# A root on ScalarE and a reciprocal on VectorE for the two scales at a kernel's first layer boundary

## The chip, the cores and the metric

The kernel runs on one core of one Trainium2 chip. The metric is the device time of one execution in microseconds. The core has a matrix engine (TensorE, PE in the profile), three engines for elementwise work (VectorE = DVE, ScalarE = ACT, GpSimd = PoolE = POOL) and a queue that issues DMAs (SyncE = SP). Each engine runs its own instruction stream in order; they wait for each other through semaphores.

## The reference, cut to what matters

Everything is float32, 272 tokens (16 meta tokens and 256 of the input) by 1024 features. The change concerns the place between the first feed-forward part and the mixer behind it:

```python
def rmsnorm(x, g):
    y = x * lax.rsqrt(jnp.mean(x * x, axis=-1, keepdims=True) + EPS)
    return y * g

h = h + 0.5 * rmsnorm(swiglu(rmsnorm(h, gn[0]), ffn_w_in, ffn_w_out), gn[1])
u = rmsnorm(h, gn[2])
y = mlstm_mixer(u, ...)          # its first step is u @ w_in
```

Two scales per token stand between the last product of the feed-forward part and the first product of the mixer: r1, one over the root of the mean square of the feed-forward output, and r2, one over the root of the mean square of the new h. Behind the mixer come a second feed-forward part and two attention layers, which the change leaves as they are.

## The kernel before, in words

Activations lie with features on the 128 partitions, as eight tiles of 128 features by 272 tokens. Weights stream in 512 KB chunks through five buffers (`raw`); for each chunk ScalarE writes the rounded upper part (`w1`, L870, a CAST) and VectorE the rest (`w2`, L1233), and a product is three TensorE matmuls (upper by upper, upper by rest, rest by upper; L370 to L372). The order of work on each engine is the order in which its program is written out by hand: functions named `tensor`, `scalar`, `vector`, `gpsimd` and `sync`, each a straight list of stages. No scheduler moves anything.

The boundary "f0" works like this. While TensorE makes the last output tile of the feed-forward part, the squares of the others have been summed. `column_sums` (L428) lets TensorE sum over features, so that sums by token stand in PSUM. VectorE's `first_scale` adds epsilon (`sst`, L1400 and L1402), takes a reciprocal of the mean square (`inv`, L1405) and begins the second sum (`msq`, L1408). PoolE's `first_power` raises `sst` to the power -0.5 (`rst`, L1898): that is r1. VectorE's `second_scale` needs r1 to finish the mean square of the new h (`msq` L1419, `msh` L1423), and PoolE's `second_power` raises it to -0.5 (L1903, into `rst2`, which the profile calls rst too): that is r2. TensorE's `both_scales` spreads each scale over the partitions with three small transposes (`spread`, L435) and runs six matmuls on a constant tile `dz` (`dense`, L386) behind the first. Then for each of the eight feature tiles VectorE scales y (`scaled`, L1426), h is added (L1435 on VectorE for two tiles, L1909 on PoolE for six), VectorE applies r2 and the gain (`tmp`, L1462), ScalarE rounds it (`u1`, L956) and VectorE makes the rest (`u2`, L1443). TensorE's `head` (L414, L416, L419) starts on the mixer's first four weight chunks tile by tile as `u1` and `u2` come.

In the mixer's stage ScalarE copies each product out of PSUM (L972, L973, L981), VectorE runs a convolution over four taps (L1537), and ScalarE takes a Silu of it (L991).

The tiles `root`, `tmp` and `line_end` of the diff are on-chip buffers that are laid out one behind the other in the order of their creation; behind `line_end` come the overlaid buffers of the stages (the feed-forward part's `h1` and `h2`, the mixer's and the attention layers' tiles).

Of the kernel before, what the change touches and what calls it, by code (L numbers as in the profile page):

```python
# [9 lines left out]
ALU = mybir.AluOpType  # L10
# [3 lines left out]
P = 128  # L14
D = 1024
KT = D // P
# [86 lines left out]
def build(nc, xT, wst, wada, vec, cst, tab, rb, nrow, outT):  # L103
    ctx = ExitStack()
    with ctx:
        def sb(name, shape, dt=F32, c=ctx):
            return c.enter_context(nc.sbuf_tensor(name, shape, dt))
# [17 lines left out]
        msh = sb("msh", [P, 4])  # L125
        msq = sb("msq", [P, 4])
        rst2 = sb("rst2", [P, 4])
        tmp = sb("tmp", [P, 4, T])
        vc = sb("vc", [P, NVEC])
        cs = sb("cs", [P, NCONST])  # L130
# [9 lines left out]
        eps0 = sb("eps0", [P, 4])  # L140
        Bt = sb("Bt", [P, NH, 384])
        rbs = sb("rbs", [NH, 32])
        sb("line_end", [P, 32])
        ps = ctx.enter_context(nc.psum_tensor("ps", [P, 8, 512], F32))
        drt = nc.dram_tensor("bias_rows", [NH, 512], F32)
        rows_dr = nc.dram_tensor("weight_rows", [2, 2 * KT, P], F32)
# [177 lines left out]
        s_zero, s_cv, s_gate, s_acol, s_swm, s_swd, s_den, s_og = signal("zp_zeroed"), signal("conv_tap"), signal("gate_step"), signal("acol_made"), signal("sw_masked"), signal("sw_weighted"), signal("den_step"), signal("og_times_y")  # L324
        s_sb, s_max, s_rec, s_cu, s_tap, s_fin = signal("sb_made"), signal("max_made"), signal("rec_made"), signal("cu_zeroed"), signal("tap_made"), signal("out_made")
        s_vrow1 = signal("second_v_rows")

        s_eps, s_one, s_xacc, s_pow, s_bias, s_accy, s_accg = signal("eps_set"), signal("ones_set"), signal("x_sq_added"), signal("pow_made"), signal("bias_row"), signal("sq_added"), signal("sqg_added")
        s_hp, s_pad, s_nrm, s_m2, s_cp = signal("h_added_pool"), signal("pads_set"), signal("p_normalised"), signal("m2_made"), signal("conv_gated")
# [23 lines left out]
        def tensor(e):  # L353
# [183 lines left out]

            def both_scales(s, n):

                e.wait_ge(s_pow.handle, at(s_pow, ("r1", s)))  # L540
                spread(("r1", s), 6, n, rst)
                dense(6)
                e.wait_ge(s_pow.handle, at(s_pow, ("r2", s)))
                spread(("r2", s), 5, n, rst2)

            def rows_of_gains(l):
# [308 lines left out]
        def scalar(e):  # L855
# [63 lines left out]
            def ffn_out(f, s, n):  # L919
                for j in range(KT):  # L920
                    split_to(C_F[f] + 2 * NF + (NF * j + NF - 1) // 8 + NW - 1)
                    key, i, i2 = ("out", s, j), j % 4, j % 2
                    src, gain, y = out_of(key, n), gain_of(s, j), yg[:, j, 0:n]
                    proj(key)
                    if j == 0:
                        e.wait_ge(s_gh.handle, 1)
                        e.activation(sqa[:, 0, 0:n], src, ACT.Square).then_inc(*tick(s_sq, (s, 0)))
                        e.activation(sqa[:, 1, 0:n], src, ACT.Square, scale=gain).then_inc(*tick(s_sqg, (s, 0)))
                        e.mul(y, src, gain).then_inc(*reading(key))
                    elif j < KT - 1:  # L930
                        if j > 4:
                            e.wait_ge(s_accy.handle, at(s_accy, (s, j - 4)))
                        e.activation(sq[:, i, 0:n], src, ACT.Square).then_inc(*tick(s_sq, (s, j)))
                        if j > 2:
                            e.wait_ge(s_accg.handle, at(s_accg, (s, j - 2)))
                        e.activation(sqg[:, i2, 0:n], src, ACT.Square, scale=gain).then_inc(*tick(s_sqg, (s, j)))
                        e.mul(y, src, gain).then_inc(*reading(key))
                    else:
                        e.wait_ge(s_accy.handle, at(s_accy, (s, 3)))
                        e.activation(sq[:, i, 0:n], src, ACT.Square).then_inc(*tick(s_sq, (s, j)))  # L940
                        e.wait_ge(s_hy.handle, at(s_hy, (s, "hy", j)))
                        e.mul(y, src, gain).then_inc(*reading(key))
# [8 lines left out]

            def normalised(s, n):

                for k in range(KT):
                    e.wait_ge(*(read(("r2", s)) if k == KT - 1 else (s_tmp.handle, at(s_tmp, (s, k)))))
                    e.copy(u1[:, k, 0:n], tmp[:, k % 4, 0:n]).then_inc(*tick(s_u1, ("a", k)))  # L956
                    if k == 1:
                        split_to(C_A + NW - 1)
# [262 lines left out]
        def vector(e):  # L1221
# [174 lines left out]
            def first_scale(s, n, eps_of):  # L1396

                tt = sum_tiles(n)
                e.wait_ge(s_colsum.handle, at(s_colsum, ("sum", s)))
                m = e.tensor_tensor(sst[:, 0:2], ps[:, 7, 0:256:128], eps_of[:, 0:2], ALU.add)  # L1400
                if n == T:
                    m = e.tensor_tensor(sst[0:16, 2:3], ps[0:16, 7, 256:257], eps_of[0:16, 2:3], ALU.add)  # L1402
                m.then_inc(*tick(s_stat, ("sst", s)))
                e.wait_ge(s_stat.handle, at(s_stat, ("sst", s)))
                e.reciprocal(inv[:, 0:len(tt)], sst[:, 0:len(tt)]).then_inc(*tick(s_stat, ("inv", s)))  # L1405
                e.wait_ge(s_stat.handle, at(s_stat, ("inv", s)))
                for j, (a, z) in enumerate(tt):
                    m = e.tensor_scalar(msq[0:z - a, j:j + 1], ps[0:z - a, 7, 128 * j + 64:128 * j + 65], inv[0:z - a, j:j + 1],  # L1408
                                        msh[0:z - a, j:j + 1], ALU.mult, ALU.add)
                m.then_inc(*reading(("sum", s)))  # L1410

            def second_scale(s, n):

                tt = sum_tiles(n)
                e.wait_ge(s_pow.handle, at(s_pow, ("r1", s)))
                e.wait_ge(s_colsum.handle, at(s_colsum, ("sumc", s)))
                e.wait_ge(*read(("sum", s)))
                for j, (a, z) in enumerate(tt):
                    m = e.tensor_scalar(msq[0:z - a, j:j + 1], ps[0:z - a, 5, 128 * j:128 * j + 1], rst[0:z - a, j:j + 1],  # L1419
                                        msq[0:z - a, j:j + 1], ALU.mult, ALU.add)  # L1420
                m.then_inc(*reading(("sumc", s)))
                e.wait_ge(*read(("sumc", s)))
                e.tensor_scalar(msh[:, 0:len(tt)], msq[:, 0:len(tt)], EPS, None, ALU.max).then_inc(*tick(s_stat, ("max", s)))  # L1423
# [12 lines left out]

            def normalised(s, nxt, n, gain, eps_of):
                first_scale(s, n, eps_of)
                second_scale(s, n)

                def lower(k):
                    e.wait_ge(s_u1.handle, at(s_u1, (nxt, k)))
                    e.tensor_tensor(u2[:, k, 0:n], tmp[:, k % 4, 0:n], u1[:, k, 0:n].bitcast(F32), ALU.subtract).then_inc(  # L1443
                        *tick(s_u2, (nxt, k)))

                e.wait_ge(s_spread.handle, at(s_spread, ("r1", s)))
                e.wait_ge(*read(("out", s, KT - 1)))
                for k in range(KT):
                    if k == 0:
                        scaled(s, 0, n)  # L1450
                        h_added(s, 0, n)
                    if k + 1 < KT:
                        scaled(s, k + 1, n)
                        if k + 1 == 4:
                            h_added(s, 4, n)
                    if k == 0:
                        e.wait_ge(s_spread.handle, at(s_spread, ("r2", s)))
                    if k in (0, 4):
                        e.wait_ge(s_hd.handle, at(s_hd, (s, k)))
                    else:  # L1460
                        e.wait_ge(s_hp.handle, at(s_hp, (s, k)))
                    m = e.scalar_tensor_tensor(tmp[:, k % 4, 0:n], hT[:, k, OFF[s]:OFF[s] + n], gain(k), ps[:, 5, 0:n],  # L1462
                                               ALU.mult, ALU.mult)
                    if k == KT - 1:
                        m.then_inc(*reading(("r2", s)))
                    else:
                        m.then_inc(*tick(s_tmp, (s, k)))
                    if k:
                        lower(k - 1)
                lower(KT - 1)  # L1470
# [385 lines left out]
        def gpsimd(e):  # L1856
# [35 lines left out]
                    e.tensor_tensor(sqa[:, 1, 0:n], sqa[:, 1, 0:n], sqg[:, j % 2, 0:n], ALU.add).then_inc(  # L1892
                        *tick(s_accg, (s, j)))

            def first_power(s, n):
                nt = len(sum_tiles(n))
                e.wait_ge(s_stat.handle, at(s_stat, ("sst", s)))
                e.tensor_tensor(rst[:, 0:nt], sst[:, 0:nt], eps3[:, 0:nt], ALU.pow).then_inc(*tick(s_pow, ("r1", s)))  # L1898

            def second_power(s, n):  # L1900
                nt = len(sum_tiles(n))
                e.wait_ge(s_stat.handle, at(s_stat, ("max", s)))
                e.tensor_tensor(rst2[:, 0:nt], msh[:, 0:nt], eps3[:, 0:nt], ALU.pow).then_inc(*tick(s_pow, ("r2", s)))  # L1903

            def h_added(s, n, ks):
                for k in ks:
                    h = hT[:, k, OFF[s]:OFF[s] + n]
# [1 line left out]
                    e.tensor_tensor(h, h, yg[:, k, 0:n], ALU.add).then_inc(*tick(s_hp, (s, k)))  # L1909

            def boundary(s, n):
                first_power(s, n)
                second_power(s, n)
                h_added(s, n, (1, 2, 3, 5, 6, 7))

            def first_row_scale(s, t):
# [241 lines left out]
```

## Time and profile before

| | us |
|---|---|
| runs, median of 3 (lowest to highest) | 784.48 (784.39 to 786.89) |
| profiled execution | 784.16 |
| its span, first to last instruction | 782.0 |
| TensorE busy | 773.6 |
| VectorE busy | 579.5 |
| ScalarE busy | 415.2 |
| PoolE busy | 117.5 |

The profile tells when each instruction ran. Its times are microseconds from the start of the span; ends of matmuls are modelled. The chain of waits that ended last is put down to TensorE for 89% of the span, to VectorE for 5%, to ScalarE for 2% and to PoolE for 0%.

### The profile page before, as it was taken

Reading aid. Unit: us, or ns where it says so; the run is one execution under the profiler, and the core shown is the slowest. Engines: PE = TensorE matmul, PEld = TensorE weight load, DVE = VectorE, ACT = ScalarE, POOL = GpSimd, SP = SyncE. Lnnn points to the kernel's source line nnn. Section 1 sums busy time; section 2 is a strip of 40 time slices with the busy share of each in tenths; the row PEclk is TensorE's granted clock in tenths of the full one; section 3 lists DMA queues with packets and bytes.
Section 4 is the critical chain, followed back from the end, with each engine's and each line's share of the span. In section 5 each row is a group of like instructions: output and inputs, shape, how many; then the busy total and the mean of one; then the engine's idle time right before and its main releaser. Section 6 shows DMA issues by size and latency. Waiting matters only on the chain.

```text
span 782.0 us, 14582 instructions
## 1 busy us (share of the span) xinstructions
PE 773.6 (99%) x5764; PEld 731.0 (93%) x5764; DVE 579.5 (74%) x926; ACT 415.2 (53%) x731; POOL 117.5 (15%) x136
## 2 busy tenths in 40 slices
PE   9999999999999999999999999999999999999997
PEld 8999999999999999889999998889999988999985
DVE  6777767799696977588888888677676768567763
ACT  7544444445247566485445443556655557455541
POOL 3800000033230000000000000010054411035510
PEclk9999999999999999999999999999999999999999
DMA  9876667696416644478878786635474571754531
GB/s 348 302 263 245 217 236 241 217 330 204 159 55 220 209 155 141 129 260 311 291 276 289 267 289 213 229 135 188 143 237 135 163 269 40 237 182 136 156 114 54
DMA packets 46114, 161.93 MB, mean 207 GB/s; under 512 B 5168, under 2 KB 6736, under 8 KB 46048
## 3 DMA queue, kind: packets, MB, share of 16 engines
q1 hardware_dynamic: 46048, 161.01, 60.4%
q8 instruction: 46, 0.75, 0.4%
q14 instruction: 20, 0.16, 0.1%
HBM read 159.91 MB, written 1.08 MB: 206 GB/s over the span
## 4 chain that ended last, share of the span: by engine, by line
PE 89%; DVE 5%; ACT 2%; issue 2%; DMA 1%; SPq 0%; POOL 0%; DVEq 0%; POOLq 0%; ACTq 0%
PE ps L370 21%; PE ps L372 20%; PE ps L371 20%; PE ps L819 5%; PE ps L817 5%; PE ps L818 5%; PE ps L759 3%; DVE w L1233 2%; PE ps L674 1%; DVE cv L1537 1%; PE ps L618 1%; PE ps L749 1%; ACT w L870 1%; PE ps L730 1%; PE ps L739 1%
## 5 line engine op out<-in xcount | busy, mean ns | idle before, releaser
L1233 DVE TENSOR_TENSOR w<-raw,w 128x1024 fp32r<-128x1024 f32 x237 | 287.9, 1222 | 129.2 <-ACT w L870 128.9
L370 PE MATMUL ps<-u,w 128*128 128x256 f32 (+1 forms) x1275 | 364.7, 286 | 0.4 <-DVE w L1233 0.4
L372 PE MATMUL ps<-u,w 128*128 128x256 f32 (+1 forms) x1275 | 360.1, 282 | 0.0
L371 PE MATMUL ps<-u,w 128*128 128x256 f32 (+1 forms) x1275 | 359.8, 282 | 0.0
L870 ACT CAST w<-raw 128x1024 fp32r<-128x1024 f32 x237 | 246.1, 1049 | 114.8 <-PE ps L372 82.1
L370 PEld LDWEIGHTS ps<-u,w 128*128 128x128 f32 x1275 | 239.4, 188 | 5.4 <-issue 3.1
L372 PEld LDWEIGHTS ps<-u,w 128*128 128x128 f32 x1275 | 239.7, 188 | 0.0
L371 PEld LDWEIGHTS ps<-u,w 128*128 128x128 f32 x1275 | 239.5, 188 | 0.1
L1932 POOL TENSOR_SCALAR Sb<-Sb,st 128x256 f32<-128x256 f32 x32 | 45.1, 1426 | 95.1 <-DVE st L1701 95.1
L1251 DVE SCALAR_TENSOR_TENSOR acc<-adr,cact,acc 128x1024 f32<-128x1024 f32 x42 | 55.7, 1340 | 0.0
L914 ACT ACTIVATE si<-tmp 128x272 f32<-128x272 f32 (+1 forms) x40 | 17.0, 425 | 66.0 <-DVE tmp L1346 66.0
L1918 POOL TENSOR_TENSOR rst<-sst,eps 128x1 f32<-128x1 f32 x8 | 4.4, 555 | 313.6 <-DVE sst L1760 313.6
L370 PE MATMUL ps<-h,w 128*128 128x272 f32 x176 | 50.8, 289 | 0.0
L371 PE MATMUL ps<-h,w 128*128 128x272 f32 x176 | 50.6, 288 | 0.0
L372 PE MATMUL ps<-h,w 128*128 128x272 f32 x176 | 50.6, 288 | 0.0
L817 PE MATMUL ps<-w,h 128*128 128x512 f32 x88 | 34.4, 390 | 0.0
L819 PE MATMUL ps<-w,h 128*128 128x512 f32 x88 | 34.3, 389 | 0.0
L818 PE MATMUL ps<-w,h 128*128 128x512 f32 x88 | 34.3, 389 | 0.0
L370 PEld LDWEIGHTS ps<-h,w 128*128 128x128 f32 x176 | 33.1, 188 | 0.1
L371 PEld LDWEIGHTS ps<-h,w 128*128 128x128 f32 x176 | 33.1, 188 | 0.0
L372 PEld LDWEIGHTS ps<-h,w 128*128 128x128 f32 x176 | 33.1, 188 | 0.0
L1350 DVE TENSOR_TENSOR hf<-si,ps 128x272 f32<-128x272 f32 (+1 forms) x40 | 17.2, 431 | 19.8 <-ACT si L914 19.8
(269 smaller groups left out, 975.8 us busy)
## 6 DMA issues: line engine op xcount, KB each, us to landing
raw<-wst SPq DMA_DIRECT2D x245, 512.0 KB, 4.4
adr<-wada SPq DMA_DIRECT2D x48, 512.0 KB, 3.7
Bt<-bias_rows SPq DMA_DIRECT2D x8, 192.0 KB, 4.1
hT<-xT SPq DMA_DIRECT2D x4, 272.0 KB, 4.3
sq<-nrow SPq DMA_DIRECT2D x2, 512.0 KB, 4.7
g2row<-weight_rows SPq DMA_DIRECT2D x2, 512.0 KB, 5.8
sq<-weight_rows SPq DMA_DIRECT2D x2, 512.0 KB, 5.4
outT<-hT SPq DMA_DIRECT2D x4, 256.0 KB, 2.0
```

The source lines that it names most:

```text
L370: e.matmul(out, a, x1, start=first, stop=False)
L371: e.matmul(out, a, x2, start=False, stop=False)
L372: return e.matmul(out, b, x1, start=False, stop=last)
L759: m = e.matmul(ps[:, b, :], xx[:, kt, 128 * t:128 * t + 128], ww, start=kt == 0 and i == 0, stop=kt == 7 and i == 2)
L817: e.matmul(out, x, a, start=i == 0, stop=False)
L818: e.matmul(out, x, b, start=False, stop=False)
L819: e.matmul(out, y, a, start=False, stop=i == n - 1).then_inc(*tick(s_proj, ("tok", s, i, t, hf)))
L870: e.copy(a, r).then_inc(*tick(s_upper, k))
L1233: e.tensor_tensor(b, r, a.bitcast(F32), ALU.subtract).then_inc(*tick(s_split, k))
L1251: e.scalar_tensor_tensor(a, w, x, a, ALU.mult, ALU.add).then_inc(*tick(s_acc, k))
L1350: e.tensor_tensor(hf[f][:, i, :], gate, out_of(ku, n), ALU.mult).then_inc(*reading(ku))
L1932: e.tensor_scalar(Sb[l][:, h % 4, t, :], Sb[l][:, h % 4, t, :], st_[l][:, h % 4, 4 + t:5 + t], None, ALU.mult).then_inc(*tick(s_nrm, (l, h ...
```

## The change

The two powers leave PoolE. r1 and r2 are each made by a square root on ScalarE (into a new tile `root`) and a reciprocal on VectorE. The widths of `column_sums` stay as they are. ScalarE also takes the root of a column of ones, behind the output tile before the last one; a table load stands ahead of it. VectorE's reciprocal for r2 stands in its stream behind the first `scaled`. PoolE keeps the six additions to h. The later boundaries keep their powers.

```diff
+        root = sb("root", [P, 12])
         tmp = sb("tmp", [P, 4, T])
...
-        sb("line_end", [P, 32])
+        sb("line_end", [P, 20])
...
             def both_scales(s, n):
-                e.wait_ge(s_pow.handle, at(s_pow, ("r1", s)))
+                e.wait_ge(s_scale.handle, at(s_scale, ("r1", s)))
                 spread(("r1", s), 6, n, rst)
                 dense(6)
-                e.wait_ge(s_pow.handle, at(s_pow, ("r2", s)))
+                e.wait_ge(s_scale.handle, at(s_scale, ("r2", s)))
                 spread(("r2", s), 5, n, rst2)
...
+                        if j == KT - 2:
+                            e.wait_ge(s_one.handle, at(s_one, "sums"))
+                            e.activation(root[:, 8:9], sums[:, 0:1], ACT.Sqrt)
...
             def normalised(s, n):
+                nt = len(sum_tiles(n))
+                e.wait_ge(s_stat.handle, at(s_stat, ("sst", s)))
+                e.activation(root[:, 0:nt], sst[:, 0:nt], ACT.Sqrt).then_inc(*tick(s_root, ("r1", s)))
+                e.wait_ge(s_stat.handle, at(s_stat, ("max", s)))
+                e.activation(root[:, 4:4 + nt], msh[:, 0:nt], ACT.Sqrt).then_inc(*tick(s_root, ("r2", s)))
...
                 e.reciprocal(inv[:, 0:len(tt)], sst[:, 0:len(tt)]).then_inc(*tick(s_stat, ("inv", s)))
+                e.wait_ge(s_root.handle, at(s_root, ("r1", s)))
+                e.reciprocal(rst[:, 0:len(tt)], root[:, 0:len(tt)]).then_inc(*tick(s_scale, ("r1", s)))
...
                     if k == 0:
                         scaled(s, 0, n)
+                        e.wait_ge(s_root.handle, at(s_root, ("r2", s)))
+                        tt = len(sum_tiles(n))
+                        e.reciprocal(rst2[:, 0:tt], root[:, 4:4 + tt]).then_inc(*tick(s_scale, ("r2", s)))
                         h_added(s, 0, n)
...
             def boundary(s, n):
-                first_power(s, n)
-                second_power(s, n)
                 h_added(s, n, (1, 2, 3, 5, 6, 7))
```

ScalarE's stream before, from the output tile before the last one (`yg`, L937) to the mixer's first convolution result (`qk`, L991). In brackets stand the semaphores that an instruction waits for.

```order
L937 ACTIVATE yg<-ps,gh 128x272
L870 CAST w<-raw 128x1024 [waits proj_done,raw_landed3]
L870 CAST w<-raw 128x1024 [waits proj_done,raw_landed4]
L940 ACTIVATE sq<-ps 128x272 [waits sq_added,proj_done]
L942 ACTIVATE yg<-ps,gh 128x272 [waits hy_made]
L956 CAST u<-tmp 128x272 [waits tmp_made] x2
...
L981 COPY vT<-ps 128x272 [waits proj_done] x2
L991 ACTIVATE qk<-cv,vc 128x272 [waits conv_tap]
```

The same stretch of ScalarE's stream now.

```order
L939 ACTIVATE yg<-ps,gh 128x272
L942 ACT_TABLE_LOAD
L942 ACTIVATE root<-sums 128x1 [waits ones_set]
L872 CAST w<-raw 128x1024 [waits proj_done,raw_landed3]
L872 CAST w<-raw 128x1024 [waits proj_done,raw_landed4]
L945 ACTIVATE sq<-ps 128x272 [waits sq_added,proj_done]
L947 ACTIVATE yg<-ps,gh 128x272 [waits hy_made]
L961 ACTIVATE root<-sst 128x3 [waits norm_step]
L963 ACTIVATE root<-msh 128x3 [waits norm_step]
L966 CAST u<-tmp 128x272 [waits tmp_made] x2
...
L991 COPY vT<-ps 128x272 [waits proj_done] x2
L1001 ACT_TABLE_LOAD
L1001 ACTIVATE qk<-cv,vc 128x272 [waits conv_tap]
```

Two table loads and three roots have come in; the second load, back to the Silu's table, stands ahead of the wait for the convolution, not behind it.

VectorE's stream before, from `inv` to the second `tmp`.

```order
L1405 RECIPROCAL inv<-sst 128x3
L1408 TENSOR_SCALAR msq<-ps,inv,msh 128x1 x2
L1408 TENSOR_SCALAR msq<-ps,inv,msh 16x1
L1419 TENSOR_SCALAR msq<-ps,rst,msq 128x1 x2
L1419 TENSOR_SCALAR msq<-ps,rst,msq 16x1
L1423 TENSOR_SCALAR msh<-msq 128x3
L1426 TENSOR_TENSOR yg<-yg,ps 128x272
L1435 TENSOR_TENSOR hT<-hT,yg 128x272
L1426 TENSOR_TENSOR yg<-yg,ps 128x272
L1462 SCALAR_TENSOR_TENSOR tmp<-hT,vc,ps 128x272
L1426 TENSOR_TENSOR yg<-yg,ps 128x272
```

The same stretch now (`rst` in the second of the two new rows is `rst2`).

```order
L1415 RECIPROCAL inv<-sst 128x3
L1417 RECIPROCAL rst<-root 128x3
L1420 TENSOR_SCALAR msq<-ps,inv,msh 128x1 x2
L1420 TENSOR_SCALAR msq<-ps,inv,msh 16x1
L1431 TENSOR_SCALAR msq<-ps,rst,msq 128x1 x2
L1431 TENSOR_SCALAR msq<-ps,rst,msq 16x1
L1435 TENSOR_SCALAR msh<-msq 128x3
L1438 TENSOR_TENSOR yg<-yg,ps 128x272
L1465 RECIPROCAL rst<-root 128x3
L1447 TENSOR_TENSOR hT<-hT,yg 128x272
L1438 TENSOR_TENSOR yg<-yg,ps 128x272
L1477 SCALAR_TENSOR_TENSOR tmp<-hT,vc,ps 128x272
```

One reciprocal stands ahead of the first `msq`, and one between the first `scaled` and the first addition to h; the rest is as it was.

## Rows read from the trace of the kernel before

**Rows 1.** The page, part 1: busy time, share of span, instructions by engine.

```profile
PE 773.6 (99%) x5764; PEld 731.0 (93%) x5764; DVE 579.5 (74%) x926; ACT 415.2 (53%) x731; POOL 117.5 (15%) x136
```

**Rows 2.** PE's list of waits: who waited for whom, us, times, longest.

```profile
PE ps L435 <- POOL rst L1903: 0.5, 1, 0.5
```

**Rows 3.** PE's timeline, the boundary: start, length, line, operation, count, [idle before].

```profile
213.01 0.59 PE L435 MATMUL ps<-cs,rst 128*128 128x128 f32 x3
213.52 0.98 PE L386 MATMUL ps<-dz 128*128 128x256 f32 x6
215.00 0.59 PE L435 MATMUL ps<-cs,rst 128*128 128x128 f32 x3 [0.49 <-POOL rst L1903]
...
216.62 0.52 PE L414 MATMUL ps<-u,w 128*128 128x272 f32 x2
...
217.67 0.77 PE L419 MATMUL ps<-u,w 128*128 128x272 f32 x4
```

**Rows 4.** POOL's timeline, the boundary.

```profile
211.79 0.86 POOL L1898 TENSOR_TENSOR rst<-sst,eps 128x3 f32<-128x3 f32 x1 [8.20 <-DVE sst L1402]
214.09 0.85 POOL L1903 TENSOR_TENSOR rst<-msh,eps 128x3 f32<-128x3 f32 x1 [1.43 <-DVE msh L1423]
...
216.55 0.77 POOL L1909 TENSOR_TENSOR hT<-hT,yg 128x272 f32<-128x272 f32 x1 [0.52 <-DVE yg L1426]
```

**Rows 5.** DVE's timeline, the boundary.

```profile
211.75 0.17 DVE L1405 RECIPROCAL inv<-sst 128x3 f32<-128x3 f32 x1
...
213.17 0.64 DVE L1419 TENSOR_SCALAR msq<-ps,rst,msq 128x1 f32<-128x1 f32 x3 [0.57 <-PE ps L428]
213.84 0.17 DVE L1423 TENSOR_SCALAR msh<-msq 128x3 f32<-128x3 f32 x1
213.92 0.44 DVE L1426 TENSOR_TENSOR yg<-yg,ps 128x272 f32<-128x272 f32 x1
...
214.76 0.43 DVE L1426 TENSOR_TENSOR yg<-yg,ps 128x272 f32<-128x272 f32 x1
215.62 0.50 DVE L1462 SCALAR_TENSOR_TENSOR tmp<-hT,vc,ps 128x272 f32<-128x272 f32 x1 [0.44 <-PE ps L435]
216.04 0.43 DVE L1426 TENSOR_TENSOR yg<-yg,ps 128x272 f32<-128x272 f32 x1
...
216.79 0.82 DVE L1443 TENSOR_TENSOR u<-tmp,u 128x272 fp32r<-128x272 f32 x1
```

**Rows 6.** ACT's timeline: the boundary, ahead of it, and the mixer's stage.

```profile
203.17 1.05 ACT L870 CAST w<-raw 128x1024 fp32r<-128x1024 f32 x1 [1.15 <-PE ps L372]
...
216.15 0.42 ACT L956 CAST u<-tmp 128x272 fp32r<-128x272 f32 x1 [4.78 <-DVE tmp L1462]
...
230.29 0.68 ACT L981 COPY vT<-ps 128x272 f32<-128x272 f32 x2
232.49 0.53 ACT L991 ACTIVATE qk<-cv,vc 128x272 f32<-128x272 f32 x1 [1.52 <-DVE cv L1537]
...
247.21 1.28 ACT L987 ACT_TABLE_LOAD   x1
248.50 0.43 ACT L987 ACTIVATE g<-g 8x272 f32<-8x272 f32 x1
```

**Rows 7.** Groups of ACT by shape: count, busy us, mean ns, idle before.

```profile
L880 ACT ACTIVATE tmp<-vc 128x8 f32<-128x8 f32 x1 | 0.2, 209 | 2.5 <-DMA vc<-vec 2.5
```

**Rows 8.** The chain that ended last, 226 to 284 us: start, length, what.

```profile
227.74 1.06 ACT w L870
...
281.28 1.38 PE ps L618 x10
```

**Rows 9.** Groups of PE: 5.0 to 6.4 us, 560 to 640 us, the whole span.

```profile
L386 PE MATMUL ps<-dz 128*128 128x256 f32 x14 | 1.8, 283 | 0.0
...
L371 PE MATMUL ps<-u,w 128*128 128x256 f32 x158 | 44.1, 279 | 0.0
...
L370 PE MATMUL ps<-h,w 128*128 128x272 f32 x176 | 50.8, 289 | 0.0
```

More of the change, by code:

```diff
@@ L326, in build @@
         s_vrow1 = signal("second_v_rows")
+        s_root, s_scale = signal("root_made"), signal("scale_made")
         s_eps, s_one, s_xacc, s_pow, s_bias, s_accy, s_accg = signal("eps_set"), signal("ones_set"), signal("x_sq_added"), signal("pow_made"), signal("bias_row"), signal("sq_added"), signal("sqg_added")
@@ L1414, in second_scale @@
                 tt = sum_tiles(n)
-                e.wait_ge(s_pow.handle, at(s_pow, ("r1", s)))
+                e.wait_ge(s_scale.handle, at(s_scale, ("r1", s)))
                 e.wait_ge(s_colsum.handle, at(s_colsum, ("sumc", s)))
@@ L1893, in squares @@
                         *tick(s_accg, (s, j)))
[L1895 to L1903, printed above, removed]
             def h_added(s, n, ks):
```

## The prediction

> **What bounds the kernel now.** I read the page's busy times first. TensorE is busy for 773.6 of 782.0 us [rows 1], so an edit on other engines counts only where TensorE stands still or where it is fed late. Next comes the list of what TensorE waited for: the boundary's second spread waited 0.5 us, once, for PoolE's power [rows 2]. That is the wait which the change is about, and it caps what the step itself can give. Then I went through the boundary engine by engine. TensorE ends its six `dz` matmuls at 213.52 + 0.98 = 214.50 and starts the spread of r2 at 215.00, 0.49 idle, released by the power [rows 3]. The power itself runs from 214.09 for 0.85 [rows 4]. VectorE has `msh` done at 213.84 + 0.17 = 214.01, does one `scaled`, an addition and a second `scaled`, and then waits 0.44 for the spread until the first `tmp` at 215.62 [rows 5]. ScalarE rounds it from 216.15 [rows 6], and the head starts at 216.62 [rows 3].
>
> Behind that the head is fed, not limited by TensorE: the matmuls on the first rest, L419 at 217.67, start when `u2` ends at 216.79 + 0.82 = 217.61 [rows 3, 5]. That `u2` ends 0.29 behind PoolE's addition (216.55 + 0.77 = 217.32) [rows 4, 5], and that addition follows the third `scaled` (216.04 + 0.43) by 0.08. So what arrives earlier at the first `tmp` is handed on through `scaled`, PoolE's addition and `u2` to TensorE. Last, the chain of waits leaves TensorE at the head's end, goes through ScalarE and VectorE from 227.74 and comes back at 281.28 [rows 8]: that stretch of the mixer has no slack to hide a later ScalarE or VectorE.
>
> **The first scale.** The power for r1 goes: 211.79 to 212.65 [rows 4]. In its place ScalarE can start the root when PoolE could, 211.79. No root is in the trace. The nearest row is a Tanh of 128x8 at 209 ns [rows 7]; the far bound is an 8x272 operation at 0.43 [rows 6]. With 0.21 the root is there at 212.00, the reciprocal at 0.17, as `inv` takes [rows 5], ends at about 212.2. The first three `msq` stand behind it now and end some 0.25 later than 212.60, where they ended before (213.17 less the idle 0.57) [rows 5]. The next `msq` waits for column sums until 213.17, so this is hidden, with 0.3 to spare; with the far bound 0.1 is left. TensorE's first spread starts at 213.01 with no idle time ahead of it [rows 3], behind the column sums; r1 is ready 0.4 before. Value: nothing on either side. If the column sums were shorter, the 0.25 would show.
>
> **The second scale.** The root can start at 214.04, 0.03 behind `msh`. ScalarE is free then: it idled 4.78 up to 216.15 [rows 6]. It ends at 214.25. The reciprocal stands behind the first `scaled`, which ends at 213.92 + 0.44 = 214.36 [rows 5]; instructions there start up to 0.08 before the one ahead ends (216.04 against 215.62 + 0.50). So it runs 214.28 to 214.45, and the spread could start 0.05 later, as it did behind the power: 214.50, just when the `dz` matmuls end. The spread moves by 0.50, and the `tmp` could move by as much. But VectorE has one instruction more: the second `scaled`, 214.76 to 215.19 before, ends 0.05 to 0.17 later, and `tmp` can start at 215.15 to 215.28 instead of 215.62. That is a gain of 0.34 to 0.47. With the far bound of 0.43 for the root, the reciprocal ends at 214.67 and the gain is 0.28. It cannot turn into a loss: root and reciprocal even then take 0.68 with the hand-over, the power and its hand-over 0.91. I take 0.40. By the cycle above it reaches the head's end and the mixer's chain whole.
>
> **The table loads.** A load takes 1.28, and the operation behind it starts 0.01 after it [rows 6]. The first new load and the dummy root (1.28 + 0.21 = 1.49) stand where ScalarE idled 1.15 ahead of the CAST at 203.17 [rows 6], which moves by 0.34. Its chunk is used several chunks later, and the CAST was waiting for a buffer, so nothing is behind it: zero. Without that cover it would be 0.34. The second load goes between the copies of V, which end at 230.97, and the first Silu at 232.49, ahead of which ScalarE idled 1.52 for the convolution [rows 6]. 1.28 fits, with 0.24 left. The load has no semaphore to wait for, so I take zero. If that cover went, all of the 1.28 would go down the chain to 281.28 [rows 8].
>
> The Trainium skill ("ScalarE: Activation LUTs", section "What ACT_TABLE_LOAD costs") gives 1283 ns for the load and about 1380 ns of drain with it, 2.66 us for a switch. The trace agrees on the load and shows no drain (247.21 + 1.28 to 248.50). By the page's sum the second switch would not fit into 1.52, 1.14 would be left over, and the time would be 785.7.
>
> **The layout.** This is the part that the words of the change do not name. All buffers behind `line_end` begin 32 bytes past a multiple of 64 now. The largest group concerned on TensorE is `h` as the moving operand: 176 matmuls in each of three lines, 528 [rows 9]. What such an address costs has one witness: `dz`, which begins 32 bytes past a multiple of 64 before too. Its 128x256 matmuls last 283 ns, those on `u` 279 [rows 9]. So the bounds are 0 and 528 x 4 ns = 2.1 us. But `dz` is both operands of its matmul at once, which may be all of the 4 ns. Below nothing I see no more than some tenths: the mixer's `SW` and `Vs` tiles come to the better address, in the 10 matmuls of a head [rows 8] at 4 ns, eight heads, 0.3. I take 1 ns each, 0.5: it is a real difference between rows, and most of it may belong to `dz` alone.
>
> The Trainium skill ("SBUF — State Buffer", section "Specifications (TRN2)") gives on-chip lines of 16 bytes. By that a shift of 32 bytes would cost nothing, and the time would be 784.1; the 283 against 279 does not bear it out, unless `dz` is special.
>
> **The sum.** -0.40 for the second scale, 0 for the first, 0 for the loads, +0.5 for the layout: +0.1 on the profiled execution, whose 784.16 (span 782.0 and 2.16 around it) is 0.32 below the median of the runs, 784.48. Predicted: 784.6, no change. Its own range is 783.8 to 785.4.
>
> **Rivals.**
> *The address costs in full.* Place: the 528 matmuls of the first feed-forward part's output. For it: 283 against 279. Against: `dz` is no ordinary matmul. Price: 2.1 - 0.4, slower by 1.7, 786.2. From 0.8 ns each it outweighs the gain; from 5 ns each it would be over 0.3%, which is more than the row shows but other buffers move as well.
> *The second table load is not hidden.* Place: ahead of the first Silu. For it: only 0.24 of cover is left, and the chain behind has no slack. Against: the load waits for nothing and ScalarE was idle. Price: 1.28 if all shows, 785.9.
> *The gain alone.* The address does nothing or helps, and the gain comes whole: 784.48 - 0.5 less up to 0.3, 783.7. For it: the waits at 215.00 and 215.62 are plain. Against: the same 283.
> *The change gains nothing.* VectorE's in-order reciprocal waits for a root later than 214.9. Then 784.5 to 785.0; no row has such a long small operation.
>
> **How the numbers follow.** Chances: forecast 0.62, with the case of no gain in it; full address cost 0.20; load not hidden 0.08; gain alone 0.10. Some 0.3%, 2.4 us, is what a measurement of this kernel can tell from no change. Of the full address cost I put 0.07 above that bound, of the load 0.02; of the gain alone 0.03 below it. So faster 0.03, same 0.88, slower 0.09. The range leaves out a tenth on either side: from 783.4 (the gain alone with a little more) to 786.4 (the address in full).
>
> **What would show it.** The second spread starts within 0.1 of the end of the first `dz` group, and the first `tmp` 0.3 to 0.5 earlier against the first column sums. The reload of the Silu's table lies wholly in ScalarE's idle time ahead of the first `qk`. The matmuls of the group on `h` last 289 or some ns more: that is the layout's term, to be read in the stretch of the first feed-forward output. I am wrong if that stretch moves by more than 2 us, if the wait behind the convolution grows, or if the median leaves 783.4 to 786.4.

## The result and the profile after

| | before | after |
|---|---|---|
| median of all runs beside each other | 784.29 (783.93 to 786.89, 20 runs) | 786.82 (786.10 to 788.51, 20 runs) |
| profiled execution | 784.16 | 786.17 |
| its span | 782.0 | 784.2 |
| TensorE busy | 773.6 | 776.3 |

The changed kernel is slower by 2.53 us, a ratio of 1.0029 [1.0023, 1.0035]. That is above the forecast of 784.6 and just outside its range of 783.4 to 786.4. Executions of one kernel differ by up to some 2 us among themselves in the first 18 us of the span, ahead of all that the change touches: in two traces of one and the same kernel, the changed one with its layout put back, the same matmul starts at 18.34 and at 20.30. What follows therefore goes by the lengths of stretches in the traces and by the intervals of the ratios.

The boundary itself did what was forecast. TensorE's timeline of the changed kernel there (start, length, line, operation, count, [idle before]), to be held against [rows 3]:

```profile
213.31 0.59 PE L437 MATMUL ps<-cs,rst 128*128 128x128 f32 x3
213.82 0.98 PE L388 MATMUL ps<-dz 128*128 128x256 f32 x6
214.81 0.59 PE L437 MATMUL ps<-cs,rst 128*128 128x128 f32 x3
...
216.44 0.52 PE L416 MATMUL ps<-u,w 128*128 128x272 f32 x2
...
217.49 0.76 PE L421 MATMUL ps<-u,w 128*128 128x272 f32 x4
```

The second spread carries no bracket any more: it starts as the `dz` group ends (213.82 + 0.98 = 214.80). From the first spread to the second it is 1.50 now, 1.99 before [rows 3]; to the head's start 3.13, 3.61 before. VectorE's timeline of the changed kernel:

```profile
212.28 0.18 DVE L1417 RECIPROCAL rst<-root 128x3 f32<-128x3 f32 x1
...
213.47 0.64 DVE L1431 TENSOR_SCALAR msq<-ps,rst,msq 128x1 f32<-128x1 f32 x3 [0.49 <-PE ps L430]
214.15 0.17 DVE L1435 TENSOR_SCALAR msh<-msq 128x3 f32<-128x3 f32 x1
...
214.59 0.17 DVE L1465 RECIPROCAL rst<-root 128x3 f32<-128x3 f32 x1
...
215.06 0.43 DVE L1438 TENSOR_TENSOR yg<-yg,ps 128x272 f32<-128x272 f32 x1
215.44 0.50 DVE L1477 SCALAR_TENSOR_TENSOR tmp<-hT,vc,ps 128x272 f32<-128x272 f32 x1
```

The first `tmp` follows `msh` by 1.29, before by 1.78 [rows 5], and the 0.44 ahead of it are gone. ScalarE's timeline of the changed kernel, from the first table load to the first Silu:

```profile
202.31 1.28 ACT L942 ACT_TABLE_LOAD   x1
203.60 0.20 ACT L942 ACTIVATE root<-sums 128x1 f32<-128x1 f32 x1
203.71 1.03 ACT L872 CAST w<-raw 128x1024 fp32r<-128x1024 f32 x1
...
212.05 0.20 ACT L961 ACTIVATE root<-sst 128x3 f32<-128x3 f32 x1 [0.37 <-DVE sst L1412]
214.35 0.20 ACT L963 ACTIVATE root<-msh 128x3 f32<-128x3 f32 x1 [2.10 <-DVE msh L1435]
...
230.09 0.68 ACT L991 COPY vT<-ps 128x272 f32<-128x272 f32 x2
230.79 1.28 ACT L1001 ACT_TABLE_LOAD   x1
232.29 0.52 ACT L1001 ACTIVATE qk<-cv,vc 128x272 f32<-128x272 f32 x1 [0.21 <-DVE cv L1552]
```

A root takes 0.20. The Silu still waits 0.21 for the convolution behind the second load, so that load costs nothing.

The loss stands elsewhere. PE's groups by shape over the whole span, in the kernel before (line, operation, tiles, shapes, count | busy us, mean ns of one | idle before):

```profile
L817 PE MATMUL ps<-w,h 128*128 128x512 f32 x88 | 34.4, 390 | 0.0
L819 PE MATMUL ps<-w,h 128*128 128x512 f32 x88 | 34.3, 389 | 0.0
...
L818 PE MATMUL ps<-w,m 128*128 128x512 f32 x64 | 24.9, 389 | 0.0
L759 PE MATMUL ps<-side,u 128*128 128x512 f32 x84 | 20.5, 395 | 0.7 <-issue 0.7
...
L818 PE MATMUL ps<-w,y 128*128 128x512 f32 x32 | 12.5, 390 | 0.0
...
L674 PE MATMUL ps<-w,u 128*128 128x512 f32 x48 | 11.9, 399 | 0.0
...
L759 PE MATMUL ps<-last_side,u 128*128 128x512 f32 x12 | 3.4, 391 | 0.0
```

The same view of the changed kernel, with the group on `h` that answers to [rows 9]:

```profile
L372 PE MATMUL ps<-h,w 128*128 128x272 f32 x176 | 51.0, 290 | 0.0
...
L819 PE MATMUL ps<-w,h 128*128 128x512 f32 x88 | 34.9, 396 | 0.0
L821 PE MATMUL ps<-w,h 128*128 128x512 f32 x88 | 34.8, 396 | 0.0
...
L820 PE MATMUL ps<-w,m 128*128 128x512 f32 x64 | 25.3, 395 | 0.0
L761 PE MATMUL ps<-side,u 128*128 128x512 f32 x84 | 20.8, 398 | 0.4 <-issue 0.4
L820 PE MATMUL ps<-w,y 128*128 128x512 f32 x32 | 12.6, 395 | 0.0
...
L761 PE MATMUL ps<-last_side,u 128*128 128x512 f32 x12 | 3.5, 396 | 0.0
```

These are the products of the second feed-forward part (`w,h`: `h` is the stationary operand, `w` the moving one), of the attention layers (`w,m`), of the mixer (`w,y`) and those with the weights kept in `side`: 264 + 192 + 96 + 96 = 648 matmuls of 512 columns. Each is 3 to 6 ns longer. No engine's wait explains it: the groups have no idle time ahead of them in either kernel, but for `side`, whose idle time shrank from 0.7 to 0.4. What differs is where `h`, `m`, `y` and `side` lie.

Holding the start of every matmul in one trace against its start in the other, from 18 us on, the stretches change by: `w,h` +1.68; `w,m` +1.21; `w,y` +0.31; `side` and `last_side` +0.38; `h,w` +0.21; the boundary -0.49; a wait for weights ahead of `side` -0.27; `u,w` -1.06. That is +2.0, as much as the two profiled executions are apart (786.17 - 784.16).

### The profile page after: what moved, and what is told of

Its sections match the earlier page's. It is cut to its first block, busy times and chain, and to the rows that moved or that the text cites. A ratio compares the mean times of both kernels' runs of the same rounds, so it can differ in the third digit from the quotient of the medians.

```text
span 784.2 us, 14587 instructions
## 1 busy us (share of the span) xinstructions
PE 776.3 (99%) x5764; PEld 730.7 (93%) x5764; DVE 579.5 (74%) x928; ACT 418.1 (53%) x736; POOL 116.2 (15%) x134
## 4 chain that ended last, share of the span: by engine, by line
PE 89%; DVE 5%; ACT 3%; issue 2%; DMA 0%; DVEq 0%; POOLq 0%; POOL 0%; SPq 0%; ACTq 0%
PE ps L372 21%; PE ps L373 20%; PE ps L374 20%; PE ps L821 5%; PE ps L819 5%; PE ps L820 5%; PE ps L761 3%; DVE w L1243 2%; PE ps L676 1%; DVE cv L1552 1%; PE ps L620 1%; ACT w L872 1%; PE ps L751 1%; PE ps L732 1%; PE ps L741 1%
```

## The experiments

Two things were to be told apart first: the change at the boundary and the layout. Then there were two theories of the layout: a matmul is longer when an operand's own address is no multiple of 64 bytes, or the distance between its two operands' addresses decides. Last, which part of the edit at the boundary gives the gain.

Addresses below are bytes per partition, modulo 256. Before: `w1`, `w2`, `h`, `m`, `y` at 0, `side` at 64, `u` at 64 where it is read from token 16 on (256 and 512 columns) and at 0 where all 272 tokens are read. After: `h`, `m`, `y` at 32, `side` at 96. "Distance" is the moving operand's address less the stationary one's, again modulo 256; that 256 is the right period is not shown.

### The changed kernel with the layout put back

```diff
-        sb("line_end", [P, 20])
+        sb("line_end", [P, 16])
```

> The changed kernel with line_end at 64 bytes, so that all buffers behind it lie where they lay before; roots, reciprocals and table loads stay. Theory A (the loss is the layout: 264 matmuls on h, 192 on m, 96 on y and 96 on side, 512 columns wide, each 5 to 6 ns longer, 3 to 3.5 us in all) expects 783.8, 0.4 to 0.5 faster than before, and 389 to 390 ns for these matmuls. Theory B (the loss is the new table loads or the waits for ScalarE) expects 786.8, as the changed kernel.

Measured: 783.66 (783.39 to 786.26, 11 runs) beside 784.71 for the kernel before, ratio 0.9994 [0.9984, 1.0005]. One buffer that nobody reads is 16 bytes shorter (32 in the built program), `tmp` and its neighbours still lie higher, and the loss is gone. This was run a second time on another chip, together with the changed kernel as it is:

> The changed kernel with line_end at 16 floats a row, so that everything laid out behind it stands where it stood, a second time, beside the changed kernel itself, for a tighter comparison. The theory (the boundary gains 0.48 us, the rest is as before): 783.6 to 783.9 us, 0.4 to 0.7 below the kernel before. The rival (the boundary's gain is lost again further on): within 0.2 us of the kernel before.

> The changed kernel unedited, on the same chip as its version with the layout put back. The theory (the layout costs 2.8 to 3.2 us beside a gain of 0.48): 786.4 to 786.9 us, 2.8 to 3.2 above the version with the layout put back. The rival (the loss belonged to the chip or the hour of the first runs): less than 1 us apart.

Measured: 784.21 (783.67 to 786.09, 12 runs) with the layout put back, 786.46 (786.14 to 787.22, 11 runs) for the changed kernel, 784.99 for the kernel before (23 runs); ratios 0.9996 [0.9987, 1.0005] and 1.0015 [1.0005, 1.0025]. The changed kernel's own forecast, 786.4 to 786.9, came true. The others missed: the medians are 2.25 apart and not 2.8 to 3.2 (the lowest runs 2.47), the version with the layout put back is above its 783.6 to 783.9, and it lies 0.78 below the kernel before and not 0.4 to 0.7. Against the kernel before the changed one loses 1.47 in the medians here and lost 2.53 the first time; the lowest runs are 2.08 and 2.17 apart, and from 18 us on the changed kernel's two traces are 2.22 and 1.99 longer than the trace of before. The order of the three kernels is the same as the first time. Groups of PE of the version with the layout put back, from its second trace:

```profile
L819 PE MATMUL ps<-w,h 128*128 128x512 f32 x88 | 34.3, 390 | 0.0
...
L820 PE MATMUL ps<-w,m 128*128 128x512 f32 x64 | 24.9, 389 | 0.0
L761 PE MATMUL ps<-side,u 128*128 128x512 f32 x84 | 20.5, 395 | 0.7 <-issue 0.7
```

They are back to the numbers of before. Held against the trace of before, matmul by matmul, everything in this trace from 18 us on is within 0.03 per group but one: the boundary is 0.48 shorter. So the change at the boundary gains 0.48 and the loss is the layout's alone. This version has the lowest median beside the kernel before in both studies, though neither interval excludes no difference.

### The kernel before with the layout shifted by 32

```diff
-        sb("line_end", [P, 32])
+        sb("line_end", [P, 40])
```

> The kernel before with line_end 32 bytes longer, nothing else. Theory A expects the loss without the gain: 784.3 + 3.0 = 787.3, and 395 ns for the 512-column matmuls on h, m, y and side. Theory B expects 784.3.

Measured: 786.96 (786.02 to 787.73) beside 784.71, ratio 1.0027 [1.0016, 1.0038]. The powers are still on PoolE; the loss is there without the change, at 2.25 and not the 3.0 expected. A group of PE:

```profile
L817 PE MATMUL ps<-w,h 128*128 128x512 f32 x88 | 34.9, 396 | 0.0
```

By stretches `w,h` changes by +1.69, `w,y` by +0.31 and `side` by +0.32, as in the changed kernel to 0.01. `u,w` changes by -1.75, which no theory foresaw; the whole from 18 us on is +1.77, and without `u,w` it would be 3.5.

### The same with 64 and with 128

```diff
-        sb("line_end", [P, 32])
+        sb("line_end", [P, 48])
```

(and `[P, 64]` for 128 bytes.)

> The kernel before with line_end 64 bytes longer. Two forms of theory A: A1 (an operand has to begin at a multiple of 64 bytes) expects 784.3 and 389 ns. A2 (what counts is how far the stationary and the moving operand lie from each other; the 48 matmuls of w on u, 64 apart, last 394 in both kernels, and those of side on u, both 64 past a multiple of 256, last 390) expects 394 to 396 ns for h, m, y and for side (then 128 against 64), 787.3.

> The kernel before with line_end 128 bytes longer: w against h, m and y 128 apart, side against u 128. If only the distance within 128 bytes counts: as before, 389 ns and 784.3. If within 256: slow again, 394 or more on h, m, y, 787.

Measured: 787.78, ratio 1.0047 [1.0035, 1.0059], and 788.04, ratio 1.0044 [1.0030, 1.0058]. With 64, `h` lies on a multiple of 64 again and the matmuls are still long; those of `side`, now at 128 against `u` at 64, are not, though A2 expected it of them too. (The expectation's 394 ns for `w` on `u` is 398 to 399 as the mean of the whole group.) Groups of PE with 64:

```profile
L817 PE MATMUL ps<-w,h 128*128 128x512 f32 x88 | 34.8, 395 | 0.0
...
L759 PE MATMUL ps<-side,u 128*128 128x512 f32 x84 | 20.5, 395 | 0.4 <-issue 0.4
...
L759 PE MATMUL ps<-last_side,u 128*128 128x512 f32 x12 | 3.4, 391 | 0.0
```

With 128 both kinds are long:

```profile
L817 PE MATMUL ps<-w,h 128*128 128x512 f32 x88 | 34.8, 396 | 0.0
...
L759 PE MATMUL ps<-last_side,u 128*128 128x512 f32 x12 | 3.4, 395 | 0.0
```

The theory of the multiple of 64 falls. Nor does 128 bring the short matmul back.

### The kernel before with everything shifted by 32

```diff
-        sb("line_start", [P, 32])
+        sb("line_start", [P, 40])
```

> The kernel before with line_start 32 bytes longer: weights, activations and stage buffers all 32 bytes higher, their distances as before. A1 (begin at a multiple of 64) expects all of the 512-column matmuls at 395 ns, 787.5 or more, as those on u join. A2 (the distance of the two operands) expects 389 ns and 784.3.

Measured: 784.79, ratio 1.0001 [0.9992, 1.0011]. Now `w1`, `w2`, `h`, `m` and `y` all begin 32 bytes past a multiple of 64, and every distance is what it was. Groups of PE:

```profile
L817 PE MATMUL ps<-w,h 128*128 128x512 f32 x88 | 34.3, 390 | 0.0
...
L759 PE MATMUL ps<-side,u 128*128 128x512 f32 x84 | 20.4, 394 | 0.7 <-issue 0.7
L674 PE MATMUL ps<-w,u 128*128 128x512 f32 x48 | 11.9, 399 | 0.0
```

The own address costs nothing; how the buffers lie against each other does. That it is the distance between a matmul's own two operands, and not that to a third buffer, is the simplest reading of this run and the next; no run tests it by itself. The witness of the prediction's layout term falls with it: `dz` lies on a multiple of 64 here, and the six `dz` matmuls at the boundary take 0.97 us, 0.98 before [rows 3].

### The weights shifted as well

```diff
+        sb("w_shift", [P, 16])
...
+        sb("w_shift_end", [P, 48])
...
-        sb("line_end", [P, 20])
+        sb("line_end", [P, 16])
```

The first two lines stand ahead of `w1` and behind `w2`, so that only these two lie 64 bytes further on, modulo 256.

> The changed kernel with the layout of before, and the weight buffers w1 and w2 moved up by 64 bytes. If the distance from stationary to moving operand decides: w on u goes from -64 to 0 (394 to 389, 48 matmuls, 0.2 us less), w on h, m and y goes from 0 to +64, which cost side on u nothing (391) when it came to that distance, so 389; in the first feed-forward part the 272-column matmuls go to -64 and may lose up to 2 ns each of some 1900 (3.5 us); the 256-column ones of the layers go from +64 to 0 and may gain. Between 782.5 and 787. If each operand's own address decides (a multiple of 64), nothing changes: 783.6.

Measured: 786.52 (786.03 to 787.94), ratio 1.0027 [1.0016, 1.0037]. Groups of PE:

```profile
L374 PE MATMUL ps<-u,w 128*128 128x256 f32 x832 | 238.7, 287 | 0.0
L375 PE MATMUL ps<-u,w 128*128 128x256 f32 x832 | 235.3, 283 | 0.0
...
L376 PE MATMUL ps<-u,w 128*128 128x272 f32 x443 | 127.0, 287 | 0.0
...
L374 PE MATMUL ps<-h,w 128*128 128x272 f32 x176 | 50.6, 288 | 0.0
...
L823 PE MATMUL ps<-w,h 128*128 128x512 f32 x88 | 34.6, 393 | 0.0
...
L821 PE MATMUL ps<-w,h 128*128 128x512 f32 x88 | 34.3, 390 | 0.0
...
L678 PE MATMUL ps<-w,u 128*128 128x512 f32 x48 | 11.6, 394 | 0.0
```

The matmuls of `w` on `u` come from distance -64 to 0 and gain 4 to 5 ns (394 against 398 to 399), as the theory of the distance has it. But the 256 columns of `u` on `w` come from 64 to 0 as well and lose 4 ns (283 against the 279 of [rows 9]), in 2,496 matmuls. And the 272 columns of `u` and `h` on `w`, which come to -64 and were expected to lose 2 ns each, gain 2 ns by their starts: the first feed-forward part's two stretches are 1.88 and 1.04 shorter than before. So the time lies in the forecast 782.5 to 787 with two of its terms the wrong way round. The distance matters, but 0 is not the best one for every form. And the three lines of one product differ now (390 to 393), which the theory doesn't explain.

### The first scale back on PoolE

```diff
-                e.wait_ge(s_stat.handle, at(s_stat, ("sst", s)))
-                e.activation(root[:, 0:nt], sst[:, 0:nt], ACT.Sqrt).then_inc(*tick(s_root, ("r1", s)))
...
+                e.tensor_tensor(rst[:, 0:nt], sst[:, 0:nt], eps3[:, 0:nt], ALU.pow).then_inc(*tick(s_pow, ("r1", s)))
```

The layout is put back here and in the next one.

> The changed kernel with the layout of before, and r1 back as a power on PoolE; r2 stays a root and a reciprocal. Theory: r1 is hidden behind the column sums on TensorE either way, all of the gain is in r2, so 783.6 as with both, and the second spread starts as far behind the first column sums. Rival: both scales carry part of the gain, 783.85.

Measured: 783.93 (783.50 to 785.98), ratio 0.9991 [0.9979, 1.0004]; the boundary is 0.48 shorter than before, as with both scales moved. The median is nearer the rival's 783.85 than the theory's 783.6, but that is less than runs differ; the trace decides, with the second spread 4.79 behind the first column sums, 4.78 in the changed kernel and 5.27 before. TensorE's timeline:

```profile
213.38 0.59 PE L437 MATMUL ps<-cs,rst 128*128 128x128 f32 x3
213.90 0.97 PE L388 MATMUL ps<-dz 128*128 128x256 f32 x6
214.89 0.59 PE L437 MATMUL ps<-cs,rst 128*128 128x128 f32 x3
```

The whole gain is the second scale's.

### Without the early root

```diff
-                        if j == KT - 2:
-                            e.wait_ge(s_one.handle, at(s_one, "sums"))
-                            e.activation(root[:, 8:9], sums[:, 0:1], ACT.Sqrt)
```

> The changed kernel with the layout of before, without the dummy root, so that the table of the root is loaded at the boundary, behind the last yg on ScalarE. Theory: the load runs in the idle time of 0.4 in part and puts r1 1.0 to 1.1 later, of which 0.5 (VectorE) is hidden; the second spread is 0.6 to 0.8 later than with the early load: 784.1 to 784.4. If a switch takes 2.66 instead of 1.28: 785.6. Rival, the early load has no worth: 783.6.

Measured: 784.57 (784.20 to 786.51), ratio 1.0001 [0.9990, 1.0012], a little above the forecast of 784.1 to 784.4. ScalarE's timeline:

```profile
211.45 1.28 ACT L958 ACT_TABLE_LOAD   x1
212.74 0.20 ACT L958 ACTIVATE root<-sst 128x3 f32<-128x3 f32 x1
```

VectorE's:

```profile
212.98 0.18 DVE L1414 RECIPROCAL rst<-root 128x3 f32<-128x3 f32 x1 [1.00 <-ACT root L958]
```

And TensorE's:

```profile
215.16 0.59 PE L437 MATMUL ps<-cs,rst 128*128 128x128 f32 x3 [0.46 <-DVE rst L1462]
```

The load stands on the boundary's path now: the second spread starts 3.61 behind the start of `sst` instead of 3.01 (3.50 before), within the 0.6 to 0.8 forecast. The early root is worth 0.60, a little more than the whole gain.

## Why the prediction was wrong

- **The first scale** (valued at nothing): right. The reciprocal ended at 212.46, `msq` still waited 0.49 for column sums, and leaving r1 on PoolE changes nothing.
- **The second scale** (-0.40, between 0.28 and 0.47): the mechanism was right, the size 0.48 to 0.49. VectorE's extra reciprocal cost nothing, where 0.05 to 0.17 was allowed: the second `scaled` ends 1.17 behind `msh` (215.06 + 0.43 less 214.32), before 1.18 [rows 5]. `tmp` starts 0.63 behind the second spread, before 0.62 [rows 3, 5], so it moved by all that the spread moved.
- **The table loads** (0): right. 0.24 of cover was forecast, 0.21 was left; the drain by which 1.14 would have been exposed doesn't show, on either side of a load: the root starts 0.01 behind its load (202.31 + 1.28 to 203.60), and the second load 0.02 behind the copies (230.09 + 0.68 to 230.79). That the mixer has no slack to hide a load that shows was not tried by any run.
- **The layout** (+0.5, bound 2.1): the step that failed, in place and in size. It was worked out on "the largest group concerned", the 528 matmuls with `h` moving. These gave +0.2. The 648 matmuls of 512 columns whose stationary operand (`h`, `m`, `y`) or moving operand (`side`) moves gave some 3.6, and the prediction never counted them, although all these buffers were known to move. The price came from `dz`, taken as a witness for an address past a multiple of 64; moving `dz` onto one changed nothing. The witness was weak from the start: behind the first one of the six `dz` matmuls at the boundary in the trace of before, all on the same address, the others last from 277 to 287 ns, so that 283 against 279 is less than they differ among themselves. What counts is how a matmul's operands lie against each other. A hint of it stood in the trace of before, in a group that the prediction didn't look at: 512 columns of `w` on `u`, 64 apart, took 399 ns, and those of `w` on `h`, 0 apart, 389 to 390. The bound of 2.1 was therefore no bound. With the stretches as measured the sum is -0.49 + 0.21 + 3.58 - 0.27 - 1.06 = +2.0, and its last two terms, both gains, the prediction didn't have either.
- The Trainium skill ("SBUF — State Buffer", section "Specifications (TRN2)") gives lines of 16 bytes. That a shift of 32 bytes is therefore free was the prediction's inference, which the page doesn't state, and the runs don't agree with it: such a shift made the kernel before 2.25 us slower by itself (786.96 against 784.71).
- **The rivals.** "The address costs in full" named 786.2, near the profiled 786.17; its place gave 0.2 of its 2.1, so the number agrees by luck. Its remark on 5 ns is a slip: 528 x 5 ns less 0.40 is 2.2, not yet 0.3% (2.4). "The gain alone", 783.7, is what the kernel gives with the layout put back (783.66 and 784.21). The other two did not happen.
- **The signs named beforehand** worked. The spread, the `tmp` and the reload showed as described, and the group on `h` was read at 290; the place for reading the layout was the wrong one: that stretch moved by 0.21, and the one sign of being wrong that came was the median, 786.82.

## What to carry to other kernels

When an edit adds or resizes an on-chip buffer, list every matmul one of whose operands moves against the other, and price them all, not the largest group alone; here 3 to 6 ns on 648 of them came to 3.6 us, seven times the edit's gain of 0.48. If a small edit gives a loss far from its place, put the layout back with a filler before doubting the edit. A table load for an added function belongs in idle time well ahead of its first use: here that is worth 0.60, and without it the gain of 0.48 would be gone.

## What was not expected of the hardware

The time of a matmul changes with the distance between its operands in the on-chip memory. For 512 columns, from the groups above and the others of the same runs (mean ns):

| distance, bytes modulo 256 | `w` on `h` | `last_side` on `u` | `w` on `u` |
|---|---|---|---|
| 0 | 389 to 390 | 390 to 391 | 394 |
| +32 | | 396 | |
| -32 | 395 to 396 | | |
| +64 | 390 to 393 | 391 | |
| -64 | 394 to 395 | | 398 to 399 |
| 128 | 395 to 396 | 395 | |

The ends of matmuls are modelled, but the steps from start to start inside these groups say the same. For `w` on `h` the mean step, without the few over 300 ns, is 227 ns at 0, 229 at +64, and 233 at -32, -64 and 128; for `w` on `u` it is 228 at 0 and 233 at -64. Why is open: no view shows the reads of the operands, and no distance between these was tried. For 256 columns the order is another (`u` on `w`: 279 at +64, 283 at 0), and for 272 columns another again: the mean step of `h` on `w` is 124 at -64, 126 at 0 and +32, 127 at +64 and 128, so the distance that is among the worst for 512 columns is the best of those tried here. Also open: the stretches of `u` on `w` that became shorter, 1.06 us in the changed kernel and 1.75 in the kernel before shifted by 32, though neither operand moved. In the changed kernel 0.83 of it lies in the second attention layer, in four groups of 48 matmuls, 5.62 us each before and 5.41 after, from its first start to the start that follows it. Inside such a group every step but the first and the last is 116 to 120 ns before and 113 or 114 after: the group runs at one pace or the other as a whole. The second trace of the changed kernel has the same four, the kernel before shifted by 32 has eight, in both layers, and that shifted by 64 has two. They stay as before when everything is shifted together and when the layout is put back. So these gains go with the layout too, but not by the distance between the two operands, which makes the distance less than the whole account. What sets the pace of a group is not shown.
